# Normalisation statistics per token: one-column sums, diagonals spread into PSUM, and the affine part on ACT

## The reference, cut to what matters

```
def rms_norm(x, g):
    y = x * lax.rsqrt(jnp.mean(x * x, axis=-1, keepdims=True) + NORM_EPS)
    return y * g
def layer_norm(x, g, b):
    mu = jnp.mean(x, axis=-1, keepdims=True)
    var = jnp.mean(jnp.square(x - mu), axis=-1, keepdims=True)
    return (x - mu) * lax.rsqrt(var + LN_EPS) * g + b
# block two, for each of its two layers l
x = layer_norm(ALPHA * x + 0.5 * swiglu_2(x, ffn_w1[l, 0], ffn_w2[l, 0]), ln_g[l, 0], ln_b[l, 0])
mix = hybrid_mixer_2(x, w_in[l], ...)
x = layer_norm(ALPHA * x + mix, ln_g[l, 1], ln_b[l, 1])
x = layer_norm(ALPHA * x + 0.5 * swiglu_2(x, ffn_w1[l, 1], ffn_w2[l, 1]), ln_g[l, 2], ln_b[l, 2])
```

## Time and profile before

| | |
|---|---|
| median of 3 runs | 3620.12 us (3619.09 to 3621.17) |
| the profiled execution | 3617.55 us, of which the span 3615.7 us |
| granted clock of TensorE, mean | 0.978 |
| PE, PEld, DVE, ACT, POOL busy | 94%, 78%, 37%, 38%, 36% of the span |
| PE's gaps in front of an opening (L788) that end with ACT L1267 | 44.7 us in 6 gaps |
| DMA | 322.05 MB, mean 89 GB/s |

### The profile page before, as it was taken

The page is one execution under the profiler, slowest core; times in us unless marked ns, Lnnn a source line. Parts: engine busy times, 40 slices in busy tenths (PEclk is TensorE's granted clock), DMA queues, the critical chain, the costliest instruction groups (busy, mean ns, idle before and its releaser), DMA issues.

```text
span 3615.7 us, 45138 instructions
## 1 busy us (share of the span) xinstructions
PE 3416.7 (94%) x16328; PEld 2818.8 (78%) x16328; DVE 1348.3 (37%) x1694; ACT 1372.9 (38%) x1814; POOL 1307.9 (36%) x547
## 2 busy tenths in 40 slices
PE   6998899899998999899999999999998989989997
PEld 4767799678887888787787888778887877878885
DVE  6753555532204220654315221242206443162214
ACT  4343344544324341325523433244323264234423
POOL 2232000134443444343343444334433433434443
PEclk9999999999999999999999999999999999999998
DMA  6331000122222222222222222222222222223222
GB/s 256 127 139 54 1 1 1 64 82 99 93 98 81 93 99 97 78 99 82 88 99 76 99 95 96 88 88 99 94 93 85 96 82 88 99 70 104 98 96 86
DMA packets 88878, 322.05 MB, mean 89 GB/s; under 512 B 9648, under 2 KB 10032, under 8 KB 88624
## 3 DMA queue, kind: packets, MB, share of 16 engines
q1 hardware_dynamic: 87424, 316.64, 25.8%
q10 hardware_dynamic: 1328, 3.67, 0.3%
HBM read 318.18 MB, written 2.10 MB: 89 GB/s over the span
## 4 chain that ended last, share of the span: by engine, by line
PE 62%; issue 27%; POOL 5%; ACT 3%; DVE 2%; POOLq 0%; DMA 0%; DVEq 0%; ACTq 0%; SPq 0%
PE ps L441 15%; PE ps L442 15%; PE ps L446 14%; POOL w_lo L418 5%; PE ps L788 5%; PE ps L865 4%; PE ps L861 4%; PE ps L862 4%; PE ps L888 1%; PE ps L887 1%; PE ps L886 1%; ACT w_hi L1013 1%; DVE X L1788 0%; DVE ps L1940 0%; DVE tmp L1911 0%
## 5 line engine op out<-in xcount | busy, mean ns | idle before, releaser
L418 POOL TENSOR_TENSOR w_lo<-raw,w_hi 128x1024 fp32r<-128x1024 f32 x543 | 1307.7, 2409 | 2288.7 <-ACT w_hi L1013 2288.5
L1013 ACT ACTIVATE w_hi<-raw 128x1024 fp32r<-128x1024 f32 x543 | 574.9, 1060 | 1546.2 <-PE ps L446 952.0
L441 PE MATMUL ps<-acts,w_hi 128*128 128x512 f32 x2848 | 1116.6, 392 | 39.1 <-DVE tmp L1945 9.7
L442 PE MATMUL ps<-acts,w_hi 128*128 128x512 f32 x2848 | 1114.5, 391 | 0.0
L446 PE MATMUL ps<-acts,w_lo 128*128 128x512 f32 x2848 | 703.4, 389 | 0.0
L441 PEld LDWEIGHTS ps<-acts,w_hi 128*128 128x128 f32 x2848 | 538.8, 189 | 157.8 <-issue 25.1
L442 PEld LDWEIGHTS ps<-acts,w_hi 128*128 128x128 f32 x2848 | 538.7, 189 | 112.0
L446 PEld LDWEIGHTS ps<-acts,w_lo 128*128 128x128 f32 x2848 | 534.6, 188 | 111.0
L1819 DVE TENSOR_TENSOR tmp<-tmp,ps 128x512 f32<-128x512 f32 x110 | 75.6, 687 | 687.3 <-PE ps L446 629.3
L861 PE MATMUL ps<-acts,w_hi 128*128 (+1 forms) x760 | 295.6, 389 | 0.0
L862 PE MATMUL ps<-acts,w_hi 128*128 (+1 forms) x760 | 295.6, 389 | 0.0
(11 more groups left out here) (370 smaller groups left out, 3359.5 us busy)
## 6 DMA issues: line engine op xcount, KB each, us to landing
raw<-stream SPq DMA_DIRECT2D x543, 512.0 KB, 3.3
ada_behind<-ada SPq DMA_DIRECT2D x32, 512.0 KB, 3.5
ada_first<-ada SPq DMA_DIRECT2D x8, 1024.0 KB, 13.2
X<-x_in ACTq DMA_DIRECT2D x1, 2048.0 KB, 8.2
out<-X SPq DMA_DIRECT2D x8, 256.0 KB, 2.0
xin<-x_in ACTq DMA_DIRECT2D x2, 768.0 KB, 7.1
xin<-x_in SPq DMA_DIRECT2D x2, 768.0 KB, 9.2
rope_sb<-rope SPq DMA_DIRECT2D x1, 1280.0 KB, 8.3
```

The costliest lines, as they stand in the source:

```text
L418: nc.gpsimd.tensor_tensor(w_lo[:, slot, :, :], raw[:, slot % RAW, :, :], f32(w_hi[:, slot, :, :]), ALU.subtract).then_inc(s_lo, 1)
L441: mm(o, w_hi[:, s, k, :], xh, start=start, stop=False, skip_group_check=True)
L442: mm(o, w_hi[:, s, k, :], xl, start=False, stop=False, skip_group_check=True)
L1013: A(w_hi[:, s, :, :], raw[:, s % RAW, :, :], ACT.Copy).then_inc(s_hi, 1)
```

## The change

The statistics are kept per token on partitions, as tiles of 128x4 (128 tokens by 4 blocks), in the new tile `mom`.

- **Sums.** `token_sums` uses a 128x128 block of the data as the weights and one column of ones as the moving operand. Four such products give 128x4 sums in one bank, SUM (bank 4) or SQUARE (bank 6). A mean norm has 16 of them (the row sums so far, the squares so far, the last row, the last square), a norm without mean 8. The waits of PE on each residual, between its last products, are gone.
- **Statistics on DVE.** Mean, its square and the variance are operations on 128x4; the inverse root is Sqrt on ACT (128x4) and a reciprocal on DVE. Ln, Exp and ACT's square of the mean are gone; the table of Sqrt is asked for ahead of the squares.
- **Spreading.** DVE makes `diagonals`, the identity times the mean (or the scale) of a block of 128 tokens, four of 128x128, and PE's `spread` multiplies ones by them into MEAN (bank 5) and SCALE (bank 7). DVE's `centre` subtracts MEAN and `unit` multiplies by SCALE, reading PSUM.
- **Affine part.** ACT writes the high part from the unit row with scale and bias (L1278 of the changed kernel) and then the row itself (L1279); DVE's affine step is gone and its low part waits for the row.
- **Order.** DVE adds the square before the residual of two steps on, and the sums follow their residual directly. ACT copies one chunk behind the squares, one behind the Sqrt, one behind row 1; behind a mixer one `done()` has moved from ahead of the last square to behind it. In `opening` the fourth slot's high-weight products for rows 0 to 2 come after row 2, ahead of the low-weight ones.

```diff
+        mom = at("mom", so, [P, 4, 4])
...
+        SUM, SQUARE, MEAN, SCALE = (ps[i] for i in (4, 6, 5, 7))
+        token_blocks = [slice(P * b, P * (b + 1)) for b in range(LAT // P)]
...
@@ -791,8 +796,9 @@
                 high_high, high_low, low_high = part(w_hi, 0), part(w_hi, 1), part(w_lo, 0)
                 late = 3
                 for k in range(KT - 2):
+                    now = SLOTS - (k < late)
                     pe.wait_ge(high, n.up())
-                    for j in range(SLOTS):
+                    for j in range(now):
                         if k == 0:
                             pe.wait_ge(s_hi, n_hi.up())
                         high_high(j, k)
@@ -800,9 +806,13 @@
                         for j in range(SLOTS):
                             low_high(j, k)
                     pe.wait_ge(low, n.now)
-                    for j in range(SLOTS):
+                    for j in range(now):
                         high_low(j, k)
                     if k == late - 1:
+                        pe.wait_ge(s_hi, n_hi.up())
+                        for i in range(late):
+                            high_high(now, i)
+                            high_low(now, i)
                         for j in range(SLOTS):
                             pe.wait_ge(s_lo, n_lo.up())
                             for i in range(late):
@@ -820,23 +830,33 @@
 
             def normed(seq, product, mean=True):
 
+                def token_sums(bank, tile, start):
+                    for b, tokens in enumerate(token_blocks):
+                        last = mm(bank[:, b:b + 1], tile[:, tokens], ones[:, 0:1], start=(start and b == 0),
+                                  stop=not start, skip_group_check=True)
+                    return last
+
+                def spread(bank, diagonals):
+                    pe.wait_ge(s_diag, n_diag.up())
+                    for tokens in token_blocks:
+                        last = mm(bank[:, tokens], ones[:, :], diagonals[:, tokens], start=True, stop=True)
+                    last.then_inc(s_bcast, 1)
+
                 for i in range(KT):
                     product(i, seq[i])
-                    if i:
-                        pe.wait_ge(s_pre, n_pre.up())
-
-                pe.wait_ge(s_pre, n_pre.up())
                 if mean:
-                    mm(ps[seq[0]][:, :], ones[:, :], X[:, seq[KT - 1], :], start=True, stop=False,
-                       skip_group_check=True)
                     pe.wait_ge(s_sadd, n_s.up(KT - 2))
-                    mm(ps[seq[0]][:, :], ones[:, :], tmp[3][:, :], start=False, stop=True,
-                       skip_group_check=True).then_inc(s_sum, 1)
+                    token_sums(SUM, tmp[3], True)
+                pe.wait_ge(s_qadd, n_q.up(KT - 2))
+                token_sums(SQUARE, tmp[2], True)
+                pe.wait_ge(s_pre, n_pre.up(KT))
+                if mean:
+                    token_sums(SUM, X[:, seq[KT - 1], :], False).then_inc(s_sum, 1)
                 pe.wait_ge(s_sqx, n_sq.up(KT))
-                mm(ps[seq[1]][:, :], ones[:, :], tmp[1][:, :], start=True, stop=False, skip_group_check=True)
-                pe.wait_ge(s_qadd, n_q.up(KT - 1))
-                mm(ps[seq[1]][:, :], ones[:, :], tmp[2][:, :], start=False, stop=True,
-                   skip_group_check=True).then_inc(s_stat, 1)
+                token_sums(SQUARE, tmp[1], False).then_inc(s_stat, 1)
+                if mean:
+                    spread(MEAN, tmp[0])
+                spread(SCALE, tmp[1])
...
-            stat, var, prod, nm = Tally(), Tally(), Tally(), Tally()
-
...
+            pre, qadd = Tally(), Tally()
+            var, prod, unit = Tally(), Tally(), Tally()
+
+            def norm(seq, g, b=None, mean=True, keep=False, chunks_behind=0):
+
+                A(epsc[:, 7:8], epsc[:, 0:1], ACT.Sqrt)
                 for i, k in enumerate(seq):
-                    if not chunks_behind:
+                    if not chunks_behind and i < KT - 1:
                         done()
                     act.wait_ge(s_pre, pre.up())
                     if i >= 2:
-                        act.wait_ge(s_qadd, qadd.up())
+                        act.wait_ge(s_qadd, qadd.now + max(1, i - 2))
                     A(tmp[i % 2][:, :], X[:, k, :], ACT.Square).then_inc(s_sqx, 1)
-                qadd.up(1)
-                for _ in range(min(chunks_behind, RAW)):
-                    done()
-                if mean:
-                    act.wait_ge(s_nm, nm.up())
-                    A(tmp[0][:, :], tmp[3][:, :], ACT.Square).then_inc(s_msq, 1)
-                act.wait_ge(s_stat, stat.up())
-                if mean:
-                    act.wait_ge(s_var, var.up())
-                    link(A(tmp[1][:, :], tmp[1][:, :], ACT.Ln, bias=epsc[:, 4:5]))
-                else:
-                    link(A(tmp[1][:, :], ps[seq[1]][:, :], ACT.Ln, scale=1.0 / D, bias=epsc[:, 0:1]))
-
-                A(tmp[1][:, :], tmp[1][:, :], ACT.Exp, scale=-0.5).then_inc(s_std, 1)
-                for _ in range(chunks_behind - RAW):
+                qadd.up(KT - 2)
+                done()
+                act.wait_ge(s_var, var.up())
+                A(mom[:, 3, :], mom[:, 2, :], ACT.Sqrt, bias=epsc[:, 4:5] if mean else epsc[:, 0:1]).then_inc(s_std, 1)
+                if chunks_behind:
                     done()
                 for k in range(KT):
-                    act.wait_ge(s_xn, xn.up())
-                    A(acts[:, k, 0, :], (tmp[2 + k % 2][:, :] if keep else X[:, k, :]),
-                      ACT.Copy).then_inc(s_xhi, 1)
+                    row = tmp[2 + k % 2][:, :] if keep else X[:, k, :]
+                    affine = dict(scale=g(k), **(dict(bias=b(k)) if b else {}))
+                    act.wait_ge(s_unit, unit.up())
+                    A(acts[:, k, 0, :], row, ACT.Identity, **affine).then_inc(s_xhi, 1)
+                    A(row, row, ACT.Identity, **affine).then_inc(s_xn, 1)
+                    if k == 1:
+                        for _ in range(chunks_behind - 2):
+                            done()
...
+            def norm(seq, residual, ready, mean=True, keep=False):
+
+                q, sums = tmp[2][:, :], tmp[3][:, :]
                 dve.wait_ge(s_dve, step.now)
                 for i, k in enumerate(seq):
+                    if i >= 2:
+                        dve.wait_ge(s_sqx, sqx.up(2 if i == 2 else 1))
+                        if i > 2:
+                            dve.wait_ge(s_qadd, qadd.now)
+                        (TT(q, tmp[0][:, :], tmp[1][:, :], ALU.add) if i == 2 else
+                         TT(q, q, tmp[(i - 1) % 2][:, :], ALU.add)).then_inc(s_qadd, 1)
+                        qadd.up()
                     ready(i)
                     residual(k).then_inc(s_pre, 1)
                     pre.up()
-                    if i:
-                        dve.wait_ge(s_sqx, sqx.up())
+                    if mean and 0 < i < KT - 1:
+                        dve.wait_ge(s_pre, pre.now)
                         if i > 1:
-                            dve.wait_ge(s_qadd, qadd.now)
-                        (CP(q, tmp[0][:, :]) if i == 1 else
-                         TT(q, q, tmp[(i - 1) % 2][:, :], ALU.add)).then_inc(s_qadd, 1)
-                        qadd.up()
+                            dve.wait_ge(s_sadd, sadd.now)
+                        TT(sums, X[:, seq[0], :] if i == 1 else sums, X[:, k, :], ALU.add).then_inc(s_sadd, 1)
+                        sadd.up()
+                sqx.up()
+
+                def diagonals(tile, column):
+                    for b, tokens in enumerate(token_blocks):
+                        last = TS(tile[:, tokens], ident[:, :], mom[:, column, b:b + 1], None, ALU.mult)
+                    last.then_inc(s_diag, 1)
+
+                def centre(k):
+                    TT(X[:, k, :], X[:, k, :], MEAN[:, :], ALU.subtract).then_inc(s_dve, 1)
+                    step.up()
+
+                row = lambda k: tmp[2 + k % 2][:, :] if keep else X[:, k, :]
+
+                def unit(k):
                     if mean:
...
+                        dve.wait_ge(s_dve, step.now - min(2, KT - 1 - k))
+                    if keep and k > 1:
+                        dve.wait_ge(s_xlo, xlo.now)
+                    TT(row(k), X[:, k, :], SCALE[:, :], ALU.mult).then_inc(s_unit, 1)
+
+                def low(k):
+                    dve.wait_ge(s_xn, xn.up())
+                    TT(acts[:, k, 1, :], row(k), f32(acts[:, k, 0, :]), ALU.subtract).then_inc(s_xlo, 1)
+                    xlo.up()
+
                 if mean:
-                    dve.wait_ge(s_sum, msq.now + 1)
-                    TS(nm, ps[seq[0]][:, :], -1.0 / D, None, ALU.mult).then_inc(s_nm, 1)
+                    dve.wait_ge(s_sum, sums_done.up())
+                    link(TS(mom[:, 0, :], SUM[:, 0:4], 1.0 / D, None, ALU.mult))
+                    diagonals(tmp[0], 0)
+                    link(TT(mom[:, 1, :], mom[:, 0, :], mom[:, 0, :], ALU.mult))
```

(21 more changed lines are left out.)

93 lines of the change are left out of this document (25 added, 68 removed).

## The result

| | before | after |
|---|---|---|
| median | 3620.0 us (6 runs beside it, 3619.1 to 3621.2) | 3633.9 us (6 runs, 3624.1 to 3641.3) |
| profiled execution | 3617.55 us, span 3615.7 us | 3641.32 us, span 3638.9 us |
| granted clock, mean | 0.978 | 0.965 |

The changed kernel is slower: its time over the kernel before is 1.0037, with a 95% interval of 1.0024 to 1.005, and the medians lie 13.9 us apart. The forecast was 3623.6 us, the same within 0.2%; the time lies at the very end of the range of 3603 to 3634, 4 us above rival C's 3629.9. Its executions also scatter over 17 us, those of the kernel before over 2 in the same set, but over 8 to 12 in the larger sets of 17 to 33 executions beside the experiments. The profiled execution of the changed kernel is the slowest of its six.

What follows compares the result with a forecast made beforehand. PE, busy 94% of the span, bounds the kernel; a norm's price is a chain of short steps. 3.9 + 2.4 + 0.3 - 0.8 (last norm) - 2.3 = +3.5 us gave 3623.6 us, range 3603 to 3634.

Steps and rivals of the forecast that it cites:

- rival C: In the norms, new steps run at half clock and DVE's prices are at their upper ends: 3629.9 us; chance 25%.
- Sums: In mean norms, 24 weight-load passes at 0.11 us give the mean's sum 2.7 us after DVE's last residual starts.
- Rival B1: One-column sums cost 0.07 us a pass, so the mean's diagonals finish before POOL begins: 3607.5 us; chance 22%.
- Diagonals shut out by POOL: In mean norms behind an FFN, both DVE diagonal sets (0.85 us per four) just miss POOL's gaps and wait.
- B2: DVE isn't shut out by POOL for operations so narrow, or gets its turn between two: 3595 us; chance 8%.
- N1: First norm: no POOL work in the way, so a change of 0.
- The spreads: In each mean norm, PE's products spreading the statistics: first 0.9 us, second 0.9 to 1.8 us at half clock.
- N4 and N7: Norms behind a mixer: POOL holds the mean's diagonals but not the second ones, +1.2 us each, +2.4 together.
- Openings: Behind FFN mean norms, POOL's low part meets the opening's low rows: 0 to 1.4 us each, taken 0.85.
- FFN norms: Three mean norms behind an FFN, later opening plus POOL's collision there: +0.85 to +1.75 us, taken +1.3 each, +3.9 together.
- N2: Norm at the end of block one, without mean: one diagonal set blocked by POOL, +0.3 us.
- Dropped waits: PE's waits per product and on the fourth slot's high part: 2.8 us at most, taken -2.3.

Runs made afterwards that it cites:

- the later add: Changed kernel with the add of the squares put back behind the residual of its step: 3627.1 us, ratio 1.0017 to the kernel before.
- the last kernel: Changed kernel with diagonals written by ACT and ten extra wide products per mean norm, the squares' add left ahead of the residual: 3608.3 us, 0.9962.

## Why the prediction was right or wrong

- **Sums, +2.7 us to the mean's sum: right in size, for other reasons.** The mean is read at T+2.3 (1479.04 against 1476.77), because the partial sums start ahead of T; a pass takes 0.11, as in the earlier trace rows. Rival B1, at 0.07, is out. T itself is late: the sum has no term for the residual that now waits for an add. That is 0.5 us in four FFN norms and 0.5 to 0.7 in the two behind a mixer.
- **Diagonals shut out by POOL: right.** The first set was to end at P+0.85 and the second at P+5.9, with P the end of the first low part; in N3 P is 1481.56, the ends are 1482.2 and 1487.55, P+0.7 and P+6.0. One costs 0.21 to 0.22. B2 is out by the copy moved behind the Sqrt. One place was missed: N1, priced at nothing "without POOL's work", had a low part in its way and is 0.7 to 1.0 us longer (0.4 to 0.6 in the three kernels where neither POOL nor the later add holds its diagonals up).
- **The spreads: wrong, and the main failure.** I priced the first at 0.9, full clock, and the second at 0.9 to 1.8. Both take 2.07 in every norm; at full clock one takes 1.16 (in the last kernel), so 0.9 was short even there. The clock before fell at E+7.3 to E+10.6 in the mean norms, and I took the moment at which PE stops as its cause, with the sums as work. They are not: it falls at E+2.4 to E+4. Rival C had this mechanism with 2.3 us for the spreads and said that it decides by PE's clock when they come; it should have been the forecast. Behind a mixer the first spread stands ahead of the reciprocal and both count in full: N4 and N7 open at E+14.3 and 14.1 instead of the 11.8 to 12.6 forecast, +3.1 and +4.2 us for the norms instead of +1.2 each.
- **Openings: +0.85 each, by rows +0.9, +0.4 and -0.2** for N3, N5 and N6. For N3 this is the size and the cause that I gave: the low row beside POOL takes 1.63, and the opening is no shorter at full clock (above). N6 has the same low row in its way and the same 24.6, but 24.8 before.
- **FFN norms: +1.3 each forecast,** +2.4, +2.5, +1.4 measured. N8 -0.8 forecast, -0.9 measured. N2 +0.3 forecast and +0.3 measured, by luck: its diagonals waited for two low parts in a row (4.2 us), its opening started 1.4 later and was 1.1 shorter.
- **Dropped waits, -2.3: right, and hidden by the clock.** Each mixer of before has two of them, the high part (0.55, first row) and L1860 (0.52, second row). Product by product, all ten profiles of kernels that contain the change gain 0.8 us at each of these two places, in both mixers: 3.3 us in all, more than forecast. The mixers are 1.2 and 0.5 longer all the same, since the clock is at half for 23.9 us in each, before for 13.7. Third and fourth row: the same 6.8 us of the first mixer (F+270.7), before and after; 25 products against 13.

```profile
1919.47 3.24 PE L788 MATMUL ps<-acts,w_hi 128*128 128x512 f32 x13 [0.55 <-ACT w_hi L1013]
1941.36 0.49 PE L441 MATMUL ps<-acts,w_hi 128*128 128x512 f32 x1 [0.52 <-DVE X L1860]
```

```profile
1775.50:1782.30 6.80, 5.77 (x25) 4.80 (x26) 4.81 (x4) 0.91 (x3) 1.32 (x1) 1.00 0.24 77
1786.60:1793.40 6.80, 5.44 (x13) 4.28 (x14) 5.15 (x4) 1.22 (x2) 1.66 (x1) 0.51 0.22 77
```

  Over the kernels that contain the change a mixer takes 456.2 to 457.4 us with 13.7 at half and 459.3 to 459.9 with 23.9. The falls come at the same four places, near 172, 203, 226 and 271 us behind F; how many of them come, and for how long, differs from kernel to kernel, and what decides it, in code that no edit touches, was not found.
- **Sum.** Forecast +3.5, measured +15.8 (+15.5) from N1 on and +13.9 by the medians. Of the 12 us missed from N1 on, about 1 is N1, 5 are N4 and N7, 2 to 3 the FFN norms, and 4 the mixers: 5 for the clock there, a term that the sum did not have, less 1 more for the dropped waits. That 3633.9 still lies in the range is luck, by 0.1 us: it is there by C's allowance of 4, and C's own terms miss the clock in the mixers too and have the diagonals at 0.28, where they took 0.22. The chances had slower by more than 0.2% at 0.25.

## What to carry to other kernels

Before moving a sum to narrow products, ask what they do to TensorE's clock: here PE was busy in every window and at half speed, and what followed, short as it was, took 2.07 us where 0.9 was priced. Small tensor_scalars from SBUF on DVE cost 0.2 us each and up to 2.4 if POOL works; put them on ACT, whose prices did not move. If a gap must stay, wide products into an unused bank can hold the clock for what follows (here they did in four norms of six), provided that none of them stands in front of a product that is waited for. And before a difference is put down to an edit, look at the stretches that it doesn't touch: here the clock's falls in the mixers hid 3.3 us of gain, and were worth up to 6.6 us between two kernels.

## What the runs showed of the hardware

- One-column products with 128x128 fp32 weights take 0.11 us a pass at full clock and 0.21 at half, and the clock fell while PE was busy with them (in one run of the kernel before, and in all norms of the changed one).
- POOL's low part and a tensor_scalar of 128x128 that start within 0.02 us of each other run one after the other; the tensor_scalars wait for the whole of it (2.22 us). ACT's operations of the same form are not touched (1.28 for four, in both sets).
- The clock's falls in the norms repeat within 0.5 us between the two profiles of a kernel, but for N7 of the kernel before (E+7.3 and E+10.6); the time ahead of N1, in code that no edit touched, scattered over 14 us between profiles.
